# Conditioning vector of a transformer block: three of eight modulation turns computed on VectorE, their weights loaded in turn with TensorE's

## The reference

```python
c_act = silu(c)                                   # one row of 2048
mod = c_act @ w_ada[l] + b_ada[l]                 # 2048 x 12288
sh1, sc1, gt1, sh2, sc2, gt2 = split(mod, 6)
h = rmsnorm(x, norm1_g) * (1.0 + sc1) + sh1       # 256 x 2048
p = h @ w_in[l]                                   # 2048 x 4384 columns
# last columns of p: low-rank inputs of decay, a and gate, and the pooling mixer;
# first 3072: r, k, v of the RWKV mixer
r, k, v, xw, xa, xg = split(p + mu * (shift(p) - p), ...)
w = -softplus(-(w0 + tanh(xw) @ w2)) - 0.5
a = sigmoid(a0 + xa @ a2)
g = sigmoid(xg) @ g2
z = (windowed mean of u) - u                      # four windows: 2, 4, 8, 16
```

## Time and profile before

| what | before |
|---|---|
| median of three runs | 2694.79 us |
| the profiled execution | 2696.14 us |
| its span | 2694.3 us |
| 1st stage, up to the last part's first product | 150.3 us |
| VectorE busy up to there | 42.8 us |
| TensorE granted clock over the span | 0.977 |

### The profile page before, as it was taken

How to read it: one execution, slowest core, us unless ns; L and a number is a source line. 1 busy time by engine, 2 the same in 40 slices (tenths; PEclk the granted TensorE clock), 3 DMA queues, 4 the chain that set the end, 5 groups by cost and what they waited for, 6 DMA issues and landing times.

```text
span 2694.3 us, 41981 instructions
## 1 busy us (share of the span) xinstructions
PE 2582.7 (96%) x18000; PEld 2240.6 (83%) x18000; DVE 1884.2 (70%) x2453; ACT 1101.1 (41%) x1312; POOL 474.8 (18%) x304
## 2 busy tenths in 40 slices
PE   6899989999999999999999999999999999999997
PEld 3678767788888888888888889899888888889996
DVE  2249863377999999999977875776547874886554
ACT  2253312234444444444455443453444443444453
POOL 0047741021000000000020776770000000000001
PEclk8899999899999999999999999999999999999998
DMA  9968567876888888888855776775757656666663
GB/s 335 337 170 234 164 216 248 280 202 182 256 249 251 250 250 250 250 250 250 250 172 138 211 205 201 212 215 156 188 189 186 163 167 187 172 172 169 187 185 116
DMA packets 744985, 570.21 MB, mean 212 GB/s; under 512 B 44608, under 2 KB 629440, under 8 KB 744672
## 3 DMA queue, kind: packets, MB, share of 16 engines
q1 hardware_dynamic: 744800, 567.52, 71.5%
HBM read 565.38 MB, written 2.10 MB: 211 GB/s over the span
## 4 chain that ended last, share of the span: by engine, by line
PE 78%; DVE 15%; DMA 2%; issue 2%; ACT 2%; POOL 1%; SPq 0%; DVEq 0%; POOLq 0%
PE bank L834 28%; PE bank L837 14%; DVE w_low L1911 4%; PE bank L801 4%; PE bank L802 3%; PE bank L803 3%; PE bank L1239 3%; PE bank L1240 3%; PE bank L1241 3%; PE bank L1087 2%; PE bank L790 2%; PE bank L871 2%; PE bank L870 2%; PE bank L872 2%; PE bank L1136 1%
## 5 line engine op out<-in xcount | busy, mean ns | idle before, releaser
L1911 DVE TENSOR_TENSOR w_low<-ring,w_high 128x2048 fp32r<-128x2048 f32 (+1 forms) x389 | 892.0, 2295 | 325.2 <-ACT w_high L1454 319.0
L834 PE MATMUL bank<-acts,w_high 128*128 128x512 f32 x4128 | 993.8, 393 | 7.3 <-DVE zs L2027 4.2
L1454 ACT ACTIVATE w_high<-ring 128x2048 fp32r<-128x2048 f32 (+1 forms) x389 | 738.2, 1901 | 382.4 <-DMA ring<-w_up 139.6
L834 PEld LDWEIGHTS bank<-acts,w_high 128*128 128x128 f32 x4128 | 760.3, 189 | 160.0 <-issue 8.3
L837 PEld LDWEIGHTS bank<-acts,w_low 128*128 128x128 f32 x4128 | 528.9, 191 | 24.6 <-DVE w_low L1911 4.9
L837 PE MATMUL bank<-acts,w_low 128*128 128x256 f32 x4128 | 536.0, 283 | 3.0 <-DVE w_low L1911 3.0
L660 POOL TENSOR_TENSOR sumf<-sqf 128x256 f32<-128x256 f32 x1 | 0.7, 742 | 786.8 <-ACT sqf L1892 786.8
L724 POOL TENSOR_TENSOR sumy<-sqy 128x256 f32<-128x256 f32 x1 | 2.1, 2094 | 761.8 <-ACT sqy L1711 761.8
L738 POOL TENSOR_SCALAR prod_g<-adg,cact 128x512 f32<-128x512 f32 x60 | 121.6, 2027 | 76.7 <-DMA adg<-w_ada 73.4
L1239 PE MATMUL bank<-w_high,hid_high 128*128 128x512 f32 x320 | 126.8, 396 | 6.7 <-DVE w_low L1911 6.7
L1240 PE MATMUL bank<-w_low,hid_high 128*128 128x512 f32 x320 | 126.3, 395 | 0.0
(11 more groups left out here) (471 smaller groups left out, 3608.8 us busy)
## 6 DMA issues: line engine op xcount, KB each, us to landing
ring<-w_in SPq DMA_DIRECT2D x176, 1024.0 KB, 5.9
ring<-w_up SPq DMA_DIRECT2D x88, 1024.0 KB, 5.9
ada<-w_ada SPq DMA_DIRECT2D x76, 1024.0 KB, 6.4
adf<-w_ada SPq DMA_DIRECT2D x44, 1024.0 KB, 5.2
ring<-w_down SPq DMA_DIRECT2D x44, 1024.0 KB, 7.4
ring<-w_out SPq DMA_DIRECT2D x16, 1024.0 KB, 6.0
adg<-w_ada SPq DMA_DIRECT2D x64, 256.0 KB, 5.6
ring<-w_mla SPq DMA_DIRECT2D x16, 1024.0 KB, 5.8
```

Of the source, the lines that this page charges most:

```text
L834: pe.matmul(o, wh[:, j], both, start=j == 0, stop=False, skip_group_check=True)
L1454: act.activation(WH[s][:, 0:WIDE[n]], ring[s][:, 0:WIDE[n]], ACT.Copy).then_inc(high_done, 1)
L1911: v.tensor_tensor(WL[s][:, 0:WIDE[n]], ring[s][:, 0:WIDE[n]], f32(WH[s][:, 0:WIDE[n]]), ALU.subtract)\
```

## The change

Of the eight turns of the first stage, five stay on TensorE (shift of part 0, scale of parts 0 to 3). The shifts of parts 1, 2 and 3 go to VectorE: each quarter lands in one of two new buffers of 8 KB a partition, `shift_rows`, laid over the place of `x`, and VectorE multiplies its four rows with four elements of the conditioning vector and adds them up in `acc_s` (`shift_piece`). TensorE sums `acc_s` over partitions in four one-column products (`shift_sums`). SyncE's list alternates the two kinds of quarters, and the second and third unit of a part move to the end of the part. The constants that only later work needs, the positions, and `rkv 1` come behind the last unit of the stage.

TensorE's order is now written tile by tile (`in_tiles`): the quarters stand between tiles of a unit. The unit `rkv 0` gets a slot of its own, is split before `in (3, 0)` (the table `SPLITS`), and is multiplied input tile by input tile: 12 before `in (3, 0)` and 4 behind `in (3, 2)`, in bank 4. `second_stage` stands behind `rkv 1` instead of `rkv 0`.

SyncE's list, its new functions and what moved:

```diff
                 a, b = IN_COLS[c:c + 2]
                 load(("in", q, c), w_in[512 * q:512 * q + 512, a:b], kt=4, cols=b - a)
 
-            for t in range(8):
-                if t % 2 == 0:
-                    ada_rows(w_ada, P * mod_col(t))
-                    if t == 0:
-                        sp.dma_start(con[:, :], consts).then_inc(inputs_landed, 16)
-                        sp.dma_start(post[:, :], pos).then_inc(inputs_landed, 16)
-                        sp.dma_start(xT[:, :, :], xT_in.rearrange("(j p) t -> p j t", p=P)).then_inc(inputs_landed, 16)
-                    in_rows(t // 2, 0)
+            def shift_rows(p, q):
+
+                k = B.up("shift") - 1
+                if k < 2:
+                    sp.wait_ge(x_taken, 1)
                 else:
-                    ada_rows(w_ada, P * mod_col(t), (0,))
-                    in_rows(t // 2, 1)
-                    ada_rows(w_ada, P * mod_col(t), (1,))
-                    in_rows(t // 2, 2)
-                    ada_rows(w_ada, P * mod_col(t), (2, 3))
-            sp.wait_ge(a_free, 32)
-            for k in range(2):
-                load(("rkv", k), cols_of(w_in, P * k))
+                    sp.wait_ge(shift_free, k - 1)
+                src = w_ada[512 * q:512 * q + 512, 512 * p:512 * p + 512]
+                sp.dma_start(AS[k % 2][:, :].rearrange("p (j n) -> p j n", j=4),
+                             src.rearrange("(j p) n -> p j n", p=P)).then_inc(shift_landed[k % 2], 16)
+
+            def scale_rows(p, quarters):
+                ada_rows(w_ada, 2048 + 512 * p, quarters)
+
+            ada_rows(w_ada, 0)
+            sp.dma_start(con[:, 0:C_FIRST], consts[:, 0:C_FIRST]).then_inc(inputs_landed, 16)
+            sp.dma_start(xT[:, :, :], xT_in.rearrange("(j p) t -> p j t", p=P)).then_inc(inputs_landed, 16)
+            for p in range(4):
+                if p:
+                    shift_rows(p, 0)
+                scale_rows(p, (0,))
+                if p:
+                    shift_rows(p, 1)
+                if p == 3:
+                    load(("rkv", 0), cols_of(w_in, 0))
+                scale_rows(p, (1,))
+                if p:
+                    shift_rows(p, 2)
+                in_rows(p, 0)
+                if p:
+                    shift_rows(p, 3)
+                scale_rows(p, (2, 3))
+                in_rows(p, 1)
+                in_rows(p, 2)
+            sp.dma_start(con[:, C_FIRST:C_WKV], consts[:, C_FIRST:C_WKV]).then_inc(rest_landed, 16)
+            sp.dma_start(post[:, :], pos).then_inc(rest_landed, 16)
+            load(("rkv", 1), cols_of(w_in, P))
             sp.wait_ge(gate_pe, 1)
             sp.dma_start(w2a2[0:64, :], w2).then_inc(extra_landed, 16)
             sp.dma_start(w2a2[64:P, :], a2).then_inc(extra_landed, 16)
             sp.dma_start(g2a[:, :], g2[0:P, :]).then_inc(extra_landed, 16)
             sp.dma_start(g2b[0:32, :], g2[P:160, :]).then_inc(extra_landed, 16)
-            sp.dma_start(pwt[:, :, :, :], pool_w.rearrange("g (k p) n -> p g k n", p=P)).then_inc(pw_landed, 16)
+            sp.wait_ge(a_free, 4 * N_SCALE)
             for k in range(2, 24):
                 load(("rkv", k), cols_of(w_in, P * k))
+                if k == 4:
+                    sp.wait_ge(unit_done, UNIT["rkv", 0] + 1)
+                    sp.dma_start(pwt[:, :, :, :], pool_w.rearrange("g (k p) n -> p g k n", p=P)).then_inc(pw_landed, 16)
                 if k == 5:
                     sp.wait_ge(gate_pe, 2)
                     sp.wait_ge(zp_ready, 8)
```

TensorE:

```diff
                                    AH[:, 4 * q + j, :], AL[:, 4 * q + j, :], q == j == m == 0, q == j == 3)
-                mm.then_inc(unit_done, 1)
-
+                if last >= len(IN_TILES[c]):
+                    mm.then_inc(unit_done, 1)
+
+            def first_rkv(js):
+
+                n = UNIT["rkv", 0]
+                if js[0] == 0:
+                    x_bank(4)
+                    pe.wait_ge(low_done, SPLIT_AT[n] + 1)
+                wh, wl = w_parts(n, 16, P)
+                for j in js:
+                    both = ACTS[:, j, :, :].rearrange("p a b -> p (a b)")
+                    pe.matmul(bank[4][:, :], wh[:, j], both, start=j == 0, stop=False, skip_group_check=True)
+                    mm = pe.matmul(bank[4][:, 0:T], wl[:, j], AH[:, j, :], start=False, stop=j == 15, skip_group_check=True)
+                if js[-1] == 15:
...
+            def shift_sums(p):
+
+                pe.wait_ge(shift_free, 4 * p)
+                o = x_bank(4)
+                for m in range(4):
+                    mm = pe.matmul(o[:, m:m + 1], acc_s[:, m * P:m * P + P], cc(C_ONES, 1), start=True, stop=True)
+                mm.then_inc(shift_full, 1)
+
+            pe.wait_ge(c_ready, 1)
             for p in range(5):
                 mod_piece()
-            pe.wait_ge(inputs_landed, 48)
+            pe.wait_ge(inputs_landed, 32)
             rms_sum(sq, DT)
             for p in range(5):
                 mod_piece()
             for q in range(3):
+                in_tiles(q, 0)
                 mod_piece()
-                for c in range(3):
+                in_tiles(q, 1, 0, 2)
+                mod_piece()
+                in_tiles(q, 1, 2)
+                in_tiles(q, 2, 0, 1)
+                for p in range(2):
                     mod_piece()
-                    in_units(q, c)
-                for p in range(6):
-                    mod_piece()
+                shift_sums(q + 1)
+                in_tiles(q, 2, 1, 2)
+                mod_piece()
+                in_tiles(q, 2, 2)
+            first_rkv(range(12))
             for c in range(3):
-                in_units(3, c)
+                in_tiles(3, c)
+            first_rkv(range(12, DT))
```

VectorE:

```diff
-                with_bias(2 * p + 2, 4 * p, 4)
-                with_bias(2 * p + 2, DT + 4 * p, 4)
+                if p:
+                    v.wait_ge(shift_full, p)
+                    v.tensor_tensor(mod[:, 4 * p:4 * p + 4], bank[4][:, 0:4], pr("b_ada", 4 * p, 4), ALU.add)\
+                        .then_inc(x_free[4], 1)
+                    B.up("x_free4")
+                    v.wait_ge(x_free[4], B.at("x_free4") + 1)
+                else:
+                    with_bias(2, 0, 4)
...
-            v.memset(raws[:, :, 0:16], 0.0)
+            v.memset(small[:, 61:62], 0.0).then_inc(x_taken, 1)
+
+            def shift_piece(p, q):
+
+                k = 4 * (p - 1) + q
+                v.wait_ge(shift_landed[k % 2], 16 * (k // 2 + 1))
+                for j in range(4):
+                    w, col = AS[k % 2][:, 512 * j:512 * j + 512], cact[:, 4 * q + j:4 * q + j + 1]
+                    if q == j == 0:
+                        ins = v.tensor_scalar(acc_s[:, :], w, col, None, ALU.mult)
+                    else:
+                        ins = v.scalar_tensor_tensor(acc_s[:, :], w, col, acc_s[:, :], ALU.mult, ALU.add)
+                    if j < 3:
+                        seq(ins)
+                ins.then_inc(shift_free, 1)
+                v.wait_ge(shift_free, k + 1)
+
+            for p in range(4):
+                if p:
+                    shift_piece(p, 0)
+                    shift_piece(p, 1)
+                    if p == 3:
+                        low_of(UNIT["rkv", 0])
+                    shift_piece(p, 2)
+                ahead("in", p, 0, to=0)
+                if p:
+                    shift_piece(p, 3)
+                modulated(p).then_inc(dve_to_pe, 1)
+                if p < 3:
+                    ahead("in", p, 2, to=0)
+            seq(v.memset(raws[:, :, 0:16], 0.0))
             for b in range(2):
-                v.memset(pa[b][:, 0:16], 0.0)
-            for p in range(4):
-                ahead("in", p, 2, to=0)
-                modulated(p).then_inc(dve_to_pe, 1)
+                seq(v.memset(pa[b][:, 0:16], 0.0))
```

149 lines of the change are left out of this document (89 added, 60 removed).

## The result

The changed kernel is slower: a median of 2703.03 us (2700.47 to 2708.78, 8 runs) against 2696.36 (2690.84 to 2702.41, 8 runs) of the kernel before, a ratio of 1.0029 with a 95% interval of 1.0016 to 1.0043. Measured once more later, beside 24 runs of before, it was 1.0017 (1.0006 to 1.0028). The forecast was 2691.9 us with a range of 2684 to 2699: the sign is wrong, and the range missed it by 4 us.

The account below looks back on a forecast made before the run. TensorE, busy 96% of the span, was taken as the bound, its first stage a weight stream with holes. -2.9 - 1.0 + 1.0 = -2.9 us from 2696.14 gave 2693.2, the median 1.35 lower: 2691.9 us, range 2684 to 2699.

Parts of the forecast that it names:

- Part 0: First product of part 0 on TensorE, forecast at 47.1 us instead of 54.0.
- M to L: From a part's first product to landing of the last quarter before the next part's scale is complete: 23.7 us.
- L to the next M: From the last quarter's landing to the next part's first product: 9.0 us, bounds 8.0 and 9.9.
- tail: Last landing to `in (3, 0)`, including 12 steps of `rkv 0`: 11.2 us; 10.6 at high clock, 12.4 at low.
- a cycle over 35 us: Self-set sign of error: one part's first product to the next's, forecast 32.7 us, outside 31 to 35.
- in (3, ·) faster by 1.0 us: Part 3's 96 products up to `in (3, 1)` take 12.0 instead of 12.96 us: -1.0 us.
- A fourth meeting in pooling: GpSimd's pooling meets a VectorE low part a fourth time, costing between 0 and 2.1 us; taken as +1.0.
- Head start of `rkv 0`: 12 of 16 steps ahead of `in (3, 0)`, 4.4 us of TensorE, counted as nothing.
- rival 3: SyncE's gated third shift quarter takes 8.03 us instead of 5.2: +5.6 us, 2700.4 us; chance 0.12.
- Rival 2: First-stage weight stream never runs dry, 4.2 us less per cycle: -15.5 us, 2679.3 us; chance 0.08.
- Rival 1: Head start of `rkv 0` counts, TensorE's saved 4.4 us reach the end: -8.3 us, 2686.5 us; chance 0.13.
- Rival 4: Gains at 150 us used up in pooling and VectorE, within 1.5 us: 2694.8 us; 0.17 with small losses.

Follow-up runs that it names:

- e1: Changed kernel with 32 and 6 extra products, results unused, ahead of TensorE's last two quarters of parts 1 to 3; 2691.8 us, ratio 0.9973.
- e2: Changed kernel with VectorE's first shift quarter of the next part moved ahead of the second and third unit's low parts; 2695.3 us, ratio 0.9989.
- e5: Changed kernel with a third buffer for shift rows, so only the fourth quarter waits for VectorE; 2692.6 us, ratio 0.9985.
- d1: Changed kernel with all three tiles of `in (q, 2)` ahead of the late quarters instead of one, no filler; 2690.72 us, ratio 0.9974.
- c1: Changed kernel with filler products ahead of the late quarters and all 16 steps of `rkv 0` behind `in (3, 2)`; 2692.61 us, ratio 0.9986.
- c3: Changed kernel with filler products, `rkv 0` behind the part, early first shift quarter and a third shift-row buffer; 2685.65 us, ratio 0.9955.
- c2: Changed kernel with filler products, `rkv 0` behind the part and VectorE's first shift quarter early; 2687.01 us, ratio 0.9961.
- the control: Kernel before the change with 6 filler products ahead of each of five later pieces between a part's units and the next part; 2706.35 us, ratio 1.0029.

## Why the prediction was wrong, point by point

**Part 0 at 47.1 us:** right (47.04), with some luck. The variants of the changed kernel do the same work ahead of part 0, and it began between 45.9 and 49.7 us in their profiled executions.

**M to L, 23.7 us:** right (23.9, 23.2, 24.2), with the lone transfer behind SyncE's wait as its reason: the third quarter left at M + 7.6 and took 5.1 us, where the row had 5.2. The section of the Trainium skill that the prediction names there, Anatomy of one DMA in DMA: Bandwidth & Descriptors, gives its figures for transfers that GpSimd issues; on SyncE's queue the row decided, and rightly.

**L to the next M, 9.0 us with a bound of 9.9; tail 11.2 with a bound of 12.4:** this is the step that failed. It measured 11.5, 11.1 and 15.7, together 9.1 us more, and `in (3, 0)` was 9.2 us later than forecast. The prediction saw that TensorE would wait and even named the low clock, but applied it to "the quarter and the short products", at 1.0 us of a possible 1.9, and left the tiles at 1.5 us and the steps of `rkv 0` at or near the high clock.

The price can be read piece by piece, start to start on TensorE, from L to `in (3, 0)`: the changed kernel (from 140.96) against e1 at the high clock (from 136.18).

| piece | changed kernel, us | e1, us | difference |
|---|---|---|---|
| quarter | 1.87 | 1.00 | 0.87 |
| shift sums | 1.73 | 0.91 | 0.82 |
| tile | 2.70 | 1.51 | 1.19 |
| row | 1.57 | 0.82 | 0.75 |
| tile | 2.70 | 1.51 | 1.19 |
| 12 steps of `rkv 0` | 5.11 | 4.24 | 0.87 |
| sum | 15.68 | 9.99 | 5.69 |

Ahead of part 1 the first four pieces decide: 3.6 us, which is all of 11.5 less 7.9. Of the 2.5 us that the forecast of 9.0 lacks there, 1.2 are the tile and 1.4 the quarter and the short products, which cost 2.4 and not 1.0 (its other terms were 0.1 too high). Ahead of part 3 everything counts, and 4.5 us are missing. The bounds were wrong for the same reason: "all at the low clock", 12.4, adds 1.8 us to the 10.6 of the high clock, but all six pieces at the low rate would be 18.3 (12 steps at 0.64 us each). The low rate of a tile could have been read in the trace of the kernel before, from the first products of its parts (0.41 us at 119.21); the earlier trace rows show it only for quarters, and there it does not simply follow a wait: 1.93 us behind waits of 0.67 and 0.77, but 1.07 behind one of 1.58.

That the low clock is the cause, and not the waits or the landings, is shown by e1 (clock 1.00, 7.9 us, with the landings 0.3 to 1.0 us later and not earlier), and within one kernel by part 1 of e2 and of e5 against their parts 0 and 2. d1 supports it, as its tiles left the slow stretch (8.9 and 7.8 us), but part of its gain is of another kind, as said there.

The sign that the prediction set itself, a cycle over 35 us, came: 35.4, 34.3 and, with the steps of `rkv 0`, 39.9 us.

**in (3, ·) faster by 1.0 us:** right, 1.35 us (150.32 to 163.81 before, 156.64 to 168.78 after). **A fourth meeting in pooling, +1.0:** right in kind, 1.9 us (37.1 to 39.0). **The distance from pooling to the keys unchanged at about 95 us:** 93.9 against 95.5. Thus the difference at the keys, +5.3 us, is +6.3 - 1.35 + 1.9 - 1.6.

**Head start of `rkv 0` worth 0:** it cost at the low clock. Moved behind, it gave 4.2 us in the tail and 2698.5 us; at the high clock (c1 against e1) the times show no worth (0.9986 and 0.9973, with intervals that overlap).

**Rivals.** The result ends on the side of rival 3, by another mechanism: the gated transfer was not late (5.1 us, and M to L as forecast). Rival 2, the stream that never runs dry, came about only with the early piece and the third buffer, in c3. Rival 1 fell: the head start is in the changed kernel, and nothing shows that it reached the end; nor is c1, which gives it up, shown to be slower than e1. Rival 4, no change within 1.5 us, is excluded by the first measurement and only just by the second, whose interval begins at 1.0006, or 1.6 us.

**From the keys to the end.** The chain's +5.3 at the keys agrees with the medians' +6.7 and, in the second measurement, +3.2 us. Profiled spans say more (+12.7). The rest arises in the scan, where the clock was lower in that execution: from the keys on, the stretches read 0.87 and 0.90 against 0.93 and 0.93 before.

```profile
301.60:355.70 54.10, 45.95 (x292) 41.14 (x293) 43.50 (x46) 20.07 (x19) 37.68 (x19) 0.87 0.44 133
355.70:538.00 182.30, 176.18 (x3649) 131.89 (x3650) 71.52 (x107) 36.82 (x67) 29.42 (x16) 0.90 0.72 242
```

In the profiled executions of all kernels here the stretch from the first scan products to the load of `w_out` took 174.0 to 185.1 us, with no order by kernel (183.6 in c1 and 175.6 in c2, which share two edits). What decides it in one execution stays open. Open as well is what moves the start of part 0 between executions (47.0 and 49.7 us in two of the changed kernel).

## What to carry to other kernels

Where an engine waits for data, look at what is queued behind the wait, not at the wait: the same 49 products took 5.93 us at one clock and 10.78 at the other, and no byte moved. Put the work that is ready ahead of the idle time and leave only what must follow the data behind it; d1 does so by moving two tiles and is 10 us faster than the changed kernel. And when a change puts new work behind a wait, price that work at the slow rate, and look for that rate in the whole trace of before: here it stood at the start of each part, in 0.41 us for a product, while the rows that were read had it only for the instructions behind the wait.

## What the runs showed that was not expected

- Filler products that compute nothing made the changed kernel 0.56% faster than it was (ratios 0.9973 and 1.0029; 0.44% against the second measurement), and 30 such products a part made the kernel before slower (1.0029). In these two kernels it paid only where ready work stood behind the idle time.
- TensorE stays at the low clock for long after it has work again, and not always equally long: from the last landing 7 us ahead of part 2 of the changed kernel (105.7 to 113) and 13 us ahead of part 3 (140.96 to 153.9).
- Short waits can bring the low clock too, and the wait just ahead does not tell: in d1 a last quarter behind waits of 1.95 and 1.66 us took 1.93 us, and one behind waits of 0.30 and 1.65 us took 1.06, with the sums behind it slow again (1.64).
- One profiled execution can be the best of its kernel: the control's trace looked as good as before, and its median was 10 us above it.
